# Six matmuls with zero weights after each V step of the segments with routing, in a mixer and expert-gather layer

## The reference

```
h   = layer_norm(x)
mix = concat(window_attention(...), gated_delta_rule(...)) @ w_out     # after one input projection
h   = layer_norm(ALPHA * h + mix)
# the expert layer: 8 heads, 16 experts each, out of 16384
expert, gates = top_k over product keys of (h @ w_query)
act = gelu(sum_d expert_u[expert] * h) * gates         # 128 experts per token
ffn = sum_k act[k] * expert_v[expert[k]]
out = layer_norm(ALPHA * h + ffn)
```

## Time and profile before

| what | value |
|---|---|
| median of three runs | 3894.4 us (3890.16 to 3905.24) |
| the profiled execution | 3923.0 us, span 3921.2 us |
| mean granted TensorE clock | 0.724 of full speed |
| busy: TensorE matmul, VectorE, GpSimd | 56%, 54%, 56% of the span |
| read from memory | 1150.46 MB |

### The profile page before, as it was taken

How to read it: one execution, slowest core, us unless ns; L and a number is a source line. 1 busy time by engine, 2 the same in 40 slices (tenths; PEclk the granted TensorE clock), 3 DMA queues, 4 the chain that set the end, 5 groups by cost and what they waited for, 6 DMA issues and landing times. The chain is left out here.

```text
span 3921.2 us, 31929 instructions
## 1 busy us (share of the span) xinstructions
PE 2195.2 (56%) x9553; PEld 1041.9 (27%) x9553; DVE 2117.9 (54%) x4846; ACT 357.3 (9%) x612; POOL 2195.0 (56%) x2079
## 2 busy tenths in 40 slices
PE   5999573754475366535653576356625762333365
PEld 2443452620241132113311332033202420100011
DVE  3021337775568754666567656755585657544400
ACT  2122201300010010001000100010001100000000
POOL 1000003575566567756776666667676666677765
PEclk9999686976686677757775777568856775566577
DMA  3224114798799789989999999889998899899997
GB/s 123 75 75 156 42 48 158 260 333 320 280 360 360 275 300 398 368 311 336 379 368 329 339 363 370 328 311 370 375 350 331 334 378 349 338 369 369 361 367 305
DMA packets 365701, 1172.72 MB, mean 299 GB/s; under 512 B 45313, under 2 KB 86354, under 8 KB 364498
## 3 DMA queue, kind: packets, MB, share of 16 engines
q0 software_dynamic: 294912, 1073.87, 73.4%
q1 hardware_dynamic: 66146, 80.92, 6.1%
q10 hardware_dynamic: 4464, 15.76, 1.0%
HBM read 1150.46 MB, written 19.96 MB: 298 GB/s over the span
## 5 line engine op out<-in xcount | busy, mean ns | idle before, releaser
L1909 DVE CUSTOM_DVE_ANT_0 U<-U,h1c 128x1024 f32<-128x1024 f32 x1024 | 1228.8, 1227 | 708.4 <-DMA U<-in_expert_u,eidx 544.5
L846 POOL DMA_INDIRECT U<-in_expert_u,eidx x1024 | 1092.1, 1066 | 469.7 <-issue 286.0
L1227 PE MATMUL bank<-V,Zb 128*32 128x512 f32 x3712 | 722.5, 890 | 920.9 <-DMA V<-in_expert_v,eidxT 805.5
L854 POOL DMA_INDIRECT V<-in_expert_v,eidxT x832 | 898.7, 1080 | 464.0 <-POOLq L852 220.7
L1227 PEld LDWEIGHTS bank<-V,Zb 128*32 128x32 f32 x3712 | 143.8, 142 | 1405.7 <-issue 1404.2
L423 PE MATMUL bank<-hT,wbuf 128*128 128x512 f32 x704 | 304.1, 595 | 0.0
L1026 PE MATMUL bank<-wq,arena 128*128 128x512 f32 x448 | 214.8, 640 | 10.1 <-PEq L1152 5.1
L840 POOL MEMSET Zb<- 128x2048 f32 x1 | 1.8, 1805 | 338.5 <-POOLq L210 338.5
L423 PEld LDWEIGHTS bank<-hT,wbuf 128*128 128x128 f32 x704 | 134.3, 191 | 169.0 <-issue 169.0
L876 POOL COPY eidx<-eidx_n 128x128 uint32<-128x128 uint32 x8 | 2.9, 358 | 284.0 <-POOLq L875 284.0
L377 DVE SCALAR_TENSOR_TENSOR ybuf<-bank,cw,ybuf 128x1023 f32<-128x1023 f32 (+2 forms) x36 | 46.1, 1281 | 201.0 <-DVEq L375 195.2
(11 more groups left out here) (264 smaller groups left out, 2711.7 us busy)
## 6 DMA issues: line engine op xcount, KB each, us to landing
arena<-in_w_out SPq DMA_DIRECT2D x56, 512.0 KB
U<-in_expert_u,eidx POOLq DMA_INDIRECT x1024
V<-in_expert_v,eidxT POOLq DMA_INDIRECT x928
proj_dram<-obuf ACTq DMA_DIRECT2D x21, 512.0 KB
raw<-proj_dram SPq DMA_DIRECT2D x8, 1344.0 KB
wbuf<-in_w_in SPq DMA_DIRECT2D x18, 512.0 KB, 3.8
wq<-in_w_query SPq DMA_DIRECT2D x4, 2048.0 KB, 16.7
xin<-in_x SPq DMA_DIRECT2D x8, 512.0 KB, 5.5
```

The lines of the kernel that those rows point to most:

```text
L846: pool.indirect_dma_start(U[:, c % NU, :], None, expert_u[0], rows(ap=eidx[:, e, c:c + 1], axis=0)).then_inc(g_u[c % NU], 16)
L854: pool.indirect_dma_start(V[:, c % NV, :], None, expert_v[0], rows(ap=eidxT[:, e, token:token + 1], axis=0)).then_inc(g_v[c % NV], 16)
L1227: last = nc.tensor.matmul(acc_ps[NSTEP * j:NSTEP * j + NSTEP, 512 * n:512 * n + 512], Zb[:, i // 4 % 2, i % 4, j, NSTEP - 1 - i:2 * NSTEP ...
L1909: ins = nc.vector.tensor_tensor_reduce(out=U[:, c % NU, :], in0=U[:, c % NU, :], in1=h1c[:, :], scale=1.0, scalar=0.0, op0=ALU.mult, op1=A ...
```

## The change

After each V step but the last of a segment, and only in the segments that also do routing (`ahead`), TensorE gets six more matmuls. Their weights are 32 columns of Zb that lie behind the column that is ever written, so they are zero. Their moving operand is 512 columns of a constant table. They add into the accumulator's first half, in the row groups 0, 1, 2, 3, 0, 1, without starting or ending an accumulation group. They wait for nothing and signal nothing. What they add is zero. `segment(..., True, True)` is called in the loop of five, so there are 5 x 31 x 6 = 930 of them.

```
+                def add_zeros():
+
+                    for i in range(6):
+                        nc.tensor.matmul(acc_ps[NSTEP * (i % 4):NSTEP * (i % 4) + NSTEP, 0:512], Zb[:, 0, 0, 0, NSTEP:2 * NSTEP],
+                                         const("level")[:, 0:512], start=False, stop=False, skip_group_check=True)
+
                         weighted(t - 1, s)
+                        if ahead and s < NSTEP - 1:
+                            add_zeros()
```

## The result

The change made the kernel slower. The median went from 3897.14 us (four runs, 3890.16 to 3905.24) to 3952.47 us (four runs, 3951.13 to 3973.71): a ratio of 1.0126, with a 95% interval of 1.0086 to 1.0165, so 55 us. The profiled execution took 3951.13 us, 28 us more than the profiled one of before, which lay above the other runs.

The account below looks back on a forecast made before the run. Gathers bound the kernel, plus holes where TensorE is late freeing V slots. Delays of 8.46 us less 2.4 us of clock give 6.1 us a segment, times five 30 us, added to 3894.4: 3924 us, range 3872 to 3962.

Parts of the forecast that it names:

- The price of six: After each V step: six zero matmuls run as two rounds, a whole V step's 1.92 us at full clock.
- The levels: After V steps 4 to 7: zeros delay the chain by 1.92, 1.92, 0.78 and 1.92 us a segment, less clock.
- behind V step 8, where I had counted nothing: Zeros after V steps 8 and 9: behind the V step that ends the hole, gathers recover, so no cost.
- VectorE's two waits: Sign in the levels: VectorE's waits of 11.10 and 7.14 us for TensorE should be about 2 us longer.
- The queries: After V steps 18 and 19: 1.92 us each, only one counted; bounds 0 and 3.84 us a segment.
- The places taken as free: Steps 0 to 3, 12 to 17 and 21 to 30: TensorE's waits or full gathers cover the zeros, no cost.
- The clock: Levels behind steps 5 and 6: zeros keep twelve cold pairs at full clock, giving back 2.4 us a segment.
- Rival B: Steps 4 to 9: clock stays up through the levels, 12 us of cold work goes, -18 us in all; chance 0.18.
- this wait as 4.15 us: In the levels, between L921 and L931: TensorE idles 4.15 us for ScalarE's copy, and the zeros do not reach it.
- The holes that the forecast listed: Third segment: low DMA share around 2225 us (0.77), around 2275 us (0.51) and at 2405 us (0.80).
- In most V steps: Whole kernel: TensorE waits 805.5 us in all for rows of V, so it is mostly ahead of the gathers.
- Instructions: 930 added matmuls, 1860 records: code fetch taken as 0, up to 3 us a segment kept in the range.

Follow-up runs that it names:

- eight: Eight zero matmuls instead of six after each V step, at the change's places, against the kernel before: 1.0183, +71 us.
- four: Four zero matmuls instead of six after each V step, one in each column group, against the kernel before: 1.0051, +20 us.
- bridge: No zeros after V steps; four zero matmuls in each level's wait for ScalarE's copy, 25 levels in all, against the kernel before: 0.9999.
- narrow: The same 930 matmuls at the same places with 32 moving columns instead of 512, against the kernel before: 1.0051, +20 us.
- zeros_idle: The zeros only after V steps 0 to 2 and 21 to 30, against the kernel before: 1.0010, +4 us.
- zeros_rest: The zeros only after V steps 3 and 9 to 17, between levels and queries, against the kernel before: 1.0035, +14 us.
- zeros_levels: The zeros only after V steps 4 to 8, where the levels of the inverse stand, against the kernel before: 1.0048, +19 us.
- zeros_queries: The zeros only after V steps 18 to 20, between the query products, against the kernel before: 1.0054, +21 us.
- six_again: The change itself run again on the third chip, against the kernel before: 1.0038, +14 us.
- narrow_twelve: Twelve matmuls of 32 moving columns after each V step instead of six of 512, third chip, against the kernel before: 1.0017, +6 us.

## Why the prediction was right

The forecast was slower by 30 us, 3924 us for a median, range 3872 to 3962. Measured were 3952.47 us. The direction was right, and so was the mechanism in the main: zeros that delay TensorE ahead of a V step make the holes of the gathers grow, and zeros in its idle time cost nothing that can be told. The size was low, 55 us by the medians. By the loops of the two traces it is 39 us, and 16 us of that in the one segment whose queries start late for a reason that the forecast didn't have; the four other segments are 3.9 us longer in the mean, less than the 6.1 us forecast. So how near the total came is in part luck.

*The price of six.* Taken as 1.92 us at full clock. Measured 1.82 us from start to start, 1.83 for eight and 0.97 for four: two rounds, shown.

*The levels.* I had 6.54 us of delay less 2.4 us of clock, 4.1 us a segment. The zeros there alone cost 19 us (8 to 30), 3.8 us a segment, and the idle time of the DMA engines in the stretch grew by 4.0 us. The sum is as forecast, the steps of it are not. The stretch became 6 us longer, and 4 of them lie behind V step 8, where I had counted nothing. I had said that VectorE's two waits would each be 2 us longer. In the third segment they are not: 11.09 us where it was 11.10, and 4.64 where it was 7.14:

```profile
2217.48 0.42 DVE L1575 TENSOR_TENSOR arena<-bank,att 128x256 f32<-128x256 f32 x1 [11.09 <-PE bank L956]
2257.76 0.69 DVE L1597 TENSOR_TENSOR raw<-raw,bank 128x512 f32<-128x512 f32 x1 [4.64 <-PE bank L932]
```

The 7.14 us had in them the late copy of 2253.30, which in the changed kernel came at the next level instead (there VectorE waits 4.99 us, before 4.18), so a single wait of one execution was a badly chosen sign. The mean length of the stretch shows the delay.

*The queries.* By the runs this is the term that was most mis-sized. I took 1.92 us a segment, counting one of two delays, with an upper bound of 3.84. The zeros there alone cost 21 us (interval 9 to 33), 4.2 us a segment. GpSimd's waits show both delays: in the third segment from 4.52 to 7.24 us and, at the next step, from 2.19 to 3.68 us, and in the means of all five. That the second wait also made a hole is not shown. In the changed kernel the idle time of the DMA engines in the queries grew in the third segment and, by 16 us, in the fifth, and in the mean of the other segments not at all.

*The places taken as free.* Steps 0 to 2 and 21 to 30 are free within the measurement (+4 us). Steps 3 and 9 to 17, which I also took as free, cost 14 us (interval 2 to 26), 2.8 us a segment. Together with the queries they would make most of what was missing. But this is the least certain of the four, since its medians differ by 4 us only.

*The clock.* Rival B lost. The clock of the levels rose from 0.80 to 0.83, not above 0.9; the zeros are over before the waits for ScalarE begin, and fill only a part of those for VectorE. In bridge they stand in the one for ScalarE, and the clock is 0.87 in the mean (four and narrow, on the same chip, have 0.82 and 0.80), without making the kernel faster than before. The Trainium skill, "TensorE: Matmul & The Clock Gate", section "HAM oscillation", has waits between bursts of matmuls as what takes the clock down; bridge agrees with that and shows that a higher clock need not give time back. The forecast also took this wait as 4.15 us. In three of the five levels of its own segment it is 0.85 us, and 4.15 was with a late copy, so B had less to win there than it seemed. On the third chip the clock of the stretch did reach 0.92 and the change was still slower by 0.38%: there the clock was not the missing part either.

*The holes that the forecast listed.* It had three places. The deepest window of its segment is a fourth, at the end, ahead of the seed:

```profile
2530.00:2540.00 10.00, 6.34 (x33) 1.28 (x32) 7.89 (x17) 0.73 (x1) 2.22 (x3) 0.68 0.35 122
```

From the end of the queries to the seed the DMA engines are idle for 12.2 us a segment before and 11.9 after. So leaving it out did no harm to the forecast, but it is about as large as the hole of the levels. "In most V steps" TensorE is ahead of the gathers was too much as well: it waits for rows in 119 of 232.

*Instructions.* I took 0. The pure form is not quite right: six narrow matmuls cost 0.5% on one chip, twelve 0.17% on another. Whether that is the added 0.2 us a step on the chain, code that is fetched, or the late copies on ScalarE, the runs leave open.

*What the forecast could not know.* The chip, or its session, decides a good part. The change costs 1.26%, and 1.5% as a sum of places, where the kernel takes 3900 to 3950 us, and 0.38% where it takes 3713 us.

## What to carry to other kernels

Filler for TensorE's clock made no kernel here faster. Behind a step whose next work is ready it is a plain delay; in the wait for ScalarE's copy it raised the clock and gained nothing; and a higher mean clock on the page says nothing about the time. In a kernel filled by its gathers, look for the windows in which the DMA engines are not full and ask which engine's lateness made each: a delay of TensorE cost time there and next to nothing where it was idle. Moving work around such a window (a V step ahead of half of the query products) gained 0.3%, the only gain. And compare segment by segment before taking a mean difference for the effect: one segment of five had 23 of the 39 us.

## What the runs showed that I had not expected

The same program differs by 6% between chips (3948 and 3713 us), and one change by a factor of three, 1.0126 and 1.0038. The chip with 3713 us is the one on which no copy of a level starts late. The late starts of ScalarE can be much longer at the queries. In the changed kernel's trace it starts a copy at 3210.06 us, 14 us after the last recorded end of the transposes on which it waits (3194.81 + 1.07), and the query products behind it wait 15.34 us:

```profile
3210.06 1.01 ACT L1411 COPY arena<-bank 128x1024 f32<-128x1024 f32 x1 [23.78 <-ACTq L1410]
```

The eight-matmul kernel has three such waits (12.71, 13.42 and 6.07 us), zeros_idle one of 13.11, narrow one of 9.10, bridge one of 7.37 and zeros_rest one of 6.96. The kernel before, zeros_levels and zeros_queries have none above 2.5 us, and six_again and narrow_twelve, on the third chip, are at 1.27 or 1.28 us throughout. Their cause was not found. That the kernel before has none may be due to the added matmuls or to chance; one trace of each kernel can't tell.
